# Output weight remainders of the last recurrence group: from VectorE to GpSimd

## What is computed

```python
def _hgrn2_mixer(h_lat, h_ctx, w_in, lb, o_gain, w_out):
    ...
    q, i_in, f_fw, f_bw, z = jnp.split(h @ w_in, 5, axis=-1)
    ...
    def readout(o, z):
        B, L = o.shape[:2]
        o = _rmsnorm(o, o_gain).reshape(B, L, D_INNER).astype(z.dtype)
        return (o * jax.nn.silu(z)) @ w_out
```

## Time and profile before

| | us |
|---|---|
| median of 3 runs | 1735.98 |
| lowest and highest run | 1735.31, 1736.64 |
| span of the profiled execution, first to last instruction | 1734.4 |
| TensorE, VectorE, ScalarE, GpSimd busy in it | 1689.0, 1184.2, 905.5, 45.4 |

### The profile page before, as it was taken

How to read it: one execution, slowest core, us unless ns; L and a number is a source line. 1 busy time by engine, 2 the same in 40 slices (tenths; PEclk the granted TensorE clock), 3 DMA queues, 4 the chain that set the end, 5 groups by cost and what they waited for, 6 DMA issues and landing times.

```text
span 1734.4 us, 34119 instructions
## 1 busy us (share of the span) xinstructions
PE 1689.0 (97%) x14251; PEld 1463.6 (84%) x14251; DVE 1184.2 (68%) x1655; ACT 905.5 (52%) x1124; POOL 45.4 (3%) x51
## 2 busy tenths in 40 slices
PE   7999999998999999999999999999999989999998
PEld 5977799987987799988988888888888868899896
DVE  4888755537588765546566877778777684687875
ACT  5666433335576443334645545455454562465772
POOL 2000000000000000000000000000000000000130
PEclk9999999999999999999999999999999999999999
DMA  8666678554648757655222222223223123352122
GB/s 199 197 221 256 216 186 200 183 193 144 182 161 316 243 150 191 192 188 178 77 86 62 87 74 62 86 62 99 62 62 98 50 98 134 116 188 66 40 73 98
DMA packets 252857, 241.90 MB, mean 139 GB/s; under 512 B 32932, under 2 KB 212224, under 8 KB 252064
## 3 DMA queue, kind: packets, MB, share of 16 engines
q1 hardware_dynamic: 250896, 233.21, 43.4%
q0 software_dynamic: 1808, 6.50, 1.3%
HBM read 238.61 MB, written 1.08 MB: 138 GB/s over the span
## 4 chain that ended last, share of the span: by engine, by line
PE 84%; DVE 6%; ACT 3%; DMA 2%; DVEq 2%; issue 1%; ACTq 1%; SPq 1%; POOLq 0%
PE pg L2657 36%; PE pg L1318 36%; PE pm L1318 7%; PE pm L1321 2%; PE pm L2657 2%; DVE ring_r L576 1%; PE pm L2660 1%; DMA ring<-in_w_ffn_up 1%; DVE ring_r L1767 1%; ACT ring_r L569 1%; DVEq L1804 1%; DMA ring<-in_w_in 0%; DMA ring<-in_hg_w_out 0%; DMA cst<-in_cst 0%; SPq L2225 0%
## 5 line engine op out<-in xcount | busy, mean ns | idle before, releaser
L576 DVE TENSOR_TENSOR ring_r<-ring,ring_r 128x2048 fp32r<-128x2048 f32 (+1 forms) x126 | 284.3, 2261 | 168.4 <-ACT ring_r L569 162.4
L2657 PE MATMUL pg<-ring_r,work_r 128*128 128x512 f32 (+1 forms) x1632 | 376.9, 391 | 8.3 <-DVEq L3176 2.7
L2657 PEld LDWEIGHTS pg<-ring_r,work_r 128*128 128x128 f32 x1632 | 300.2, 190 | 76.6 <-issue 9.6
L1318 PE MATMUL pg<-ring_r,work_r 128*128 128x512 f32 (+3 forms) x1280 | 354.6, 383 | 4.2 <-DVEq L1768 2.1
L569 ACT ACTIVATE ring_r<-ring 128x2048 fp32r<-128x2048 f32 (+1 forms) x126 | 237.6, 1890 | 196.4 <-DMA ring<-in_w_ffn_up 79.2
L2657 PE MATMUL pg<-work_r,ring_r 128*128 128x256 f32 x2688 | 318.8, 281 | 0.5 <-DVE ring_r L576 0.5
L2657 PEld LDWEIGHTS pg<-work_r,ring_r 128*128 128x128 f32 x2688 | 317.3, 188 | 2.0 <-DVE ring_r L576 1.1
L1318 PE MATMUL pg<-ring_r 128*128 128x512 f32 (+3 forms) x752 | 284.2, 378 | 1.1 <-DVEq L831 1.1
L1318 PEld LDWEIGHTS pg<-ring_r,work_r 128*128 128x128 f32 x1280 | 235.4, 188 | 48.6 <-DVEq L1768 4.1
L1318 PE MATMUL pg<-work_r,ring_r 128*128 128x512 f32 (+1 forms) x976 | 264.0, 360 | 1.0 <-POOLq L943 1.0
L1318 PEld LDWEIGHTS pg<-work_r,ring_r 128*128 128x128 f32 x976 | 173.0, 189 | 27.9 <-POOLq L943 1.5
(11 more groups left out here) (402 smaller groups left out, 1798.5 us busy)
## 6 DMA issues: line engine op xcount, KB each, us to landing
ring<-in_w_in SPq DMA_DIRECT2D x36, 1024.0 KB, 5.3
ring<-in_hg_w_in SPq DMA_DIRECT2D x48, 512.0 KB, 4.0
ring<-in_w_ffn_gate SPq DMA_DIRECT2D x44, 512.0 KB, 4.1
ring<-in_w_ffn_up SPq DMA_DIRECT2D x44, 512.0 KB, 5.4
ring<-in_w_ffn_down SPq DMA_DIRECT2D x22, 1024.0 KB, 4.9
ring<-in_ada_w SPq DMA_DIRECT2D x16, 1024.0 KB, 9.3
ring<-in_hg_w_in SPq DMA_DIRECT2D x64, 256.0 KB, 3.0
ring<-in_w_out SPq DMA_DIRECT2D x12, 1024.0 KB, 5.9
```

What stands on the lines that cost most here:

```text
L576: W.low_done(V.tensor_tensor(lo, W.raw(i, name)[:, 0:lo.shape[1]], W.hi(i, name).bitcast(f32), ALU.subtract))
L1318: return T.matmul(out_, lhsT, rhs, start=first, stop=last)
L2657: return T.matmul(out_, lhsT, rhs, start=first, stop=last)
```

## The change

GpSimd gets the remainders of hgo1, hgo2 and hgo3, ahead of its wait for the end of the last group. VectorE makes none of them any more, and waits for hgo3's before it makes hgo4's, which keeps the count in order. ScalarE makes hgo1's high part before the keys of level 2 and not behind them.

```diff
@@ second_pool
             pool.dma_start(oT[:, 2048:2048 + INNER * BLOCK], d["hmask"]).then_inc(loaded_mask, 16)
+            for name, last in (("hgo1", "hgo0"), ("hgo2", "hgo1"), ("hgo3", "hgo2")):
+                MP.wait_low(pool, last)
+                MP.wait_high(pool, name)
+                G.tensor_tensor(MP.lo(name), MP.raw(name), MP.hi(name).bitcast(f32), ALU.subtract)
+                MP.low_done(pool.drain())
             h_free.wait(pool, NG - 1)
@@ second_act, group
                 if prev is not None:
                     out_transposed(prev)
+                if not nxt:
+                    piece_high("hgo1")
                 keys_of_level(n, b, 2)
                 if nxt:
                     high(*nxt, "q0")
                     evac(*nxt, "gf")
                 else:
-                    piece_high("hgo1")
                     heads_high(4, 6)
@@ second_dve, group
                     else:
-                        for name in {2: ("hgo1",), 4: ("hgo2",)}.get(lev, ()):
-                            piece_low(name)
                         heads_low(*((2, 3), (3, 4), (4, 5), (5, 7), (7, 8), (8, 10), (10, 12))[lev])
...
                 if not nxt:
-                    piece_low("hgo3")
                     heads_low(12, 14)
...
                 else:
+                    MP.wait_low(dve, "hgo3")
                     piece_low("hgo4")
```

## The result

The changed kernel takes 1747.84 us (median of 5, 1745.87 to 1749.54) against 1735.31 of the kernel before beside it (median of 5): +12.5 us, ratio 1.0067 with an interval of 1.0056 to 1.0078 (the ratios are estimates of their own and differ a little from the quotient of the medians). Measured again on the chip of later experiments it took 1746.87 (4 runs) against 1736.07 (18 runs), ratio 1.0059 (1.0044 to 1.0074), +10.8. The forecast was 1744.5 and the range ended at 1746.5: slower as forecast, and by more than the range held. The profiled execution is the fastest of the first five: 1745.87 us with a span of 1744.0 us.

The account below looks back on a forecast made before the run. TensorE, 97% busy, bounds the kernel, with 5.6 us of waiting to win. VectorE's stops behind GpSimd put the last grow 9.2 us later, less 0.7 hidden: +8.5 on 1735.98 gives 1744.5; range 1736.5 to 1746.5.

Parts of the forecast that it names:

- The rows of L2093: Attention part: a two-column VectorE instruction takes 0.17 us, but 0.36 beside a GpSimd subtraction, ending when GpSimd's does.
- the upper bound: VectorE instructions with two SBUF inputs wait until GpSimd's instruction ends; net +8.5 us.
- GpSimd's 4.59 us: Estimated length of each GpSimd subtraction of 128x2048, from the line through two narrower ones.
- The cost of hgo1: GpSimd's first subtraction stops level 1's join; level 4 starts at 1411.28 instead of 1409.43.
- ScalarE's move: hgo1's high part before the level-2 keys ends at 1396.4, covered by ScalarE's idle time: cost nothing.
- the gain without contention: Rival: two-input VectorE instructions run on beside GpSimd; 0.7 us less, 1735.3; chance 0.15.
- the two joins named: VectorE joins made to wait for GpSimd: 1397.36's ends at 1402.6 (hgo1), a later one at 1415.1 (hgo2).
- its own sum: Whole group, VectorE waiting for each GpSimd subtraction: level 5 5.6 us later, last grow 9.2, net +8.5.
- The 0.7 "back" at the second transposes: After the last grow: an earlier 0.52 us wait for ScalarE is now hidden, giving 0.7 us back.
- The order of the third stop: Level 5: GpSimd makes hgo3's remainder behind the whole grow, 1424.7 to 1429.3; last grow 9.2 us later.
- the prediction's worst order: hgo3's subtraction slips between the halves of level 5's grow, level 6 itself waits: 9.5 us, 1745.5.
- Its upper end: Top of the forecast range for the run time: 1746.5, a us above the worst order of stops.

Follow-up runs that it names:

- the kernel with filling: Changed kernel with hgo3's remainder back on VectorE and 15 unread TensorE matmuls ahead of head 5: 1739.99 us, ratio 1.0021 to the kernel before.
- the kernel with both fillings: Changed kernel plus unread TensorE matmuls, 15 ahead of head 5 and 11 behind head 7: 1746.02 us, ratio 1.0059 to the kernel before.

## Why the prediction was wrong in size

**Right.** The rows of L2093 carried over to instructions with two SBUF inputs, and the take of the upper bound with it: the mechanism was the one forecast. GpSimd's 4.59 us were 4.53 to 4.63. The cost of hgo1 was worked out as 1.85 at level 4 and is 1.5 with hgo1 alone. ScalarE's move costs nothing, the gain without contention is 0.7. hgo1's and hgo2's stops fell on the two joins named. In the repeated profile the order of events was the same.

**The term that was missing.** The prediction said "The clock granted was 1.00 in this stretch, and should stay", though its own sum had TensorE waiting 4 us ahead of head 5 and 3 ahead of head 8. Heads 5 and 6 stood in the sum at 5.4 us, 0.3 under the 5.7 that the rows of before give; they took 8.56 and 7.30 in the two profiles. This step failed: the sum put at nothing what a wait of TensorE costs behind its end. Set against head 0 in the first profile:

| start behind head 0, us | before | forecast, later by | measured, later by |
|---|---|---|---|
| level 3 | 14.9 | 2.45 | 2.05 |
| level 5 | 26.3 | 5.6 | 8.0 |
| last scaling | 32.2 | 9.2 | 10.0 |
| transposes behind it | 34.8 | 9.2 | 11.6 |
| last transposes | 56.2 | 8.5 | 10.8 |

Level 5 is 8.0 late, 2.9 of it heads 5 and 6 at half clock (8.56 less the 5.7 with filling); without that it would be 5.1, near the 5.6 of the forecast, and the kernel with filling has 5.2. The third subtraction then started while VectorE was idle, so it stopped the level-5 scaling by 2.1 us only, and the last scaling is 0.8 later than forecast. Head 8 at half clock kept the transposes waiting 1.5 more. 8.5 + 0.8 + 1.5 = 10.8, what the group has. The 0.7 "back" at the second transposes is there: the twelve run as one row.

**The order of the third stop.** A second step was off, and the clock hid it. The sum has the level-5 scaling start at 1422.35, hgo3's high part ready at 1422.9, and GpSimd wait until the whole pair is over. With level 5 on time again (the kernel with both fillings) GpSimd got in between the halves and the pair took 6.77 us; with hgo3 alone it took 6.70. That is the prediction's worst order. With both fillings level 5 comes 2.8 us sooner than in the changed kernel, and yet the last scaling stands 9.9 us later than before, where it stood 10.0: what the clock takes at heads 5 and 6 and what the longer stop takes stand for each other. Only the loss at level 6 and head 8 comes on top either way (1.5 us in the first profile). That the last scaling was so near its forecast of 9.2 in the first profile is in part luck, since a late level 5 shortened the stop.

**The range.** Its upper end took the worst order of the stops and nothing for the clock; the rest of the way to the median (1747.84 where the profiled run has 1745.87) is spread between runs. In the second profile the run is 1.5 us slower than in the first and its group 0.9 longer, so more than half of that difference lies in this stretch. Whether all of the 1745.7 to 1749.5 comes from the clock and the third stop was not shown, since two of nine runs were profiled.

**Lock and clock.** The join beside a GpSimd subtraction was stopped (4.79 for 1.15 us), the join beside a GpSimd write was not (1.17), and the copy with one input in PSUM and one in SBUF was not (0.45). The Trainium skill ("SBUF — State Buffer", "Who interferes with whom") states these three cases so, and the runs agree. How many SBUF inputs of VectorE it takes was not varied: L2093, whose one tensor input lies in SBUF, ended with GpSimd too. The granted clock was 0.64 and 0.70 behind waits of 3.62 and 2.85 us. The Trainium skill ("TensorE: Matmul & The Clock Gate", "HAM oscillation — how this bites in real kernels") says that idle gaps can throw TensorE back to the slow clock, so that the work after the gap starts slow; the windows above agree.

## What to carry to other kernels

Before work goes to GpSimd, ask whether it reads SBUF and what VectorE does in that time: instructions with two SBUF inputs stand still until it ends, and then 4.6 us on GpSimd cost more than 2.3 on VectorE, as here. The subtractions that GpSimd makes in the attention part stand beside VectorE work with a PSUM input that keeps its length (L2129 in the earlier trace rows) and beside L2093, which does not; what they cost in all was not measured. Wherever a forecast has TensorE waiting for several us, put a term for the clock behind the wait, and take from a kernel with the work left out what there is to win at all: here 0.7 us.

## What was not expected of the hardware

GpSimd gets its turn between two VectorE instructions that stand back to back: the pair of 2.35 us took 6.70 to 6.77. The prediction had this only as its worst order. A wait of TensorE that is filled with unread matmuls can make the whole shorter (63.7 to 61.2 us for the group), and the same filling, with a second one behind head 7, won almost nothing (67.0 to 66.5) where it moved VectorE's scaling into GpSimd's next instruction.
